# Last attention pair of a decoder step: the output layer's first operands are loaded ahead of row 7's blocks, two half tiles begin before the last values product, and the weights of the next pair are scaled behind row 1's maxima

## The chip, the cores and the metric

The kernel runs on one core of one Trainium2 chip. The metric is the device time of one execution in microseconds (us); lower is better.

## The reference

Two layers over a prompt of 1024 tokens and 8 single decode tokens: first a gated linear recurrence, then an attention layer. The change lies in the attention layer, of which this is the core:

```python
k, v = jnp.split(rms_norm(h, norm_kv) @ w_kv, 2, axis=-1)          # shared keys and values, 16 heads of 64
q, gate = jnp.split(rms_norm(x, norm_g) @ w_in, 2, axis=-1)
...
logits = jnp.where(mask, s + (c_q[..., :, None] - c_t[..., None, :]), -jnp.inf)
p = jax.nn.softmax(logits, axis=-1)
o = jnp.einsum('bhqk,bkhd->bqhd', p, v_all)
...
return x + (o * jax.nn.silu(gate)) @ w_o                           # the output layer
```

The decode tokens attend to a paged cache of 1024 keys each. All data are fp32.

## The kernel before

The first half of the run is the recurrent layer, which the change does not touch. The attention layer goes over eight pairs of heads, p = 0 to 7. A pair has eight **rows** of 128 queries (row i has i + 1 blocks of 128 keys). For a row TensorE computes scores (`scores`, L2446), VectorE adds the forget terms and takes the minimum (`row_max`, L1794 and L1798; in rows 4 to 7 also L1787), ScalarE makes the softmax (`soft`, L1274 and L1283), and the weights are transposed: rows 0 to 3 on TensorE (`turn_rows`, L2453, copied out by `turn_a` L1290 and `turn_v` L1807), rows 4 to 7 by VectorE (`turn_blocks`, L1819), stored to DRAM by SyncE (`store_row`, L679) and loaded back (`load_row`, L690). `weighted(p, m)` (L2472) multiplies rows 2m and 2m+1 with the values. `weighted(p, 3)` needs row 7's loaded blocks and stands in the next pair's row 2.

Between these the order of each engine is written by hand. In pairs 0 to 6 TensorE fills its gaps with the projections of the next pair, `kq_n` and `vg_n`: units of four matmuls (recorded as eight) at L2134, each added or copied out of one of two banks (VectorE L1451, ScalarE L1024), so that unit n waits for the taking of unit n-2. Unit 0 of `kq` waits until VectorE has scaled `w_k` and `w_q` (`scale_w`, L477, one instruction each); unit 1 waits until GpSimd has made sums of the scaled weights (`sums_of_kq`, L813 to L816, four instructions that wait for both scalings). In pair 7 there is no next pair, and `last` puts parts of the **output layer** into the gaps: `y_part(n, lo, hi)` (L2646) accumulates heads lo to hi-1 of half tile n, n = 0, 1, 2 in banks 0, 1, 7. Its first three heads wait for the semaphore `early_b`, which counts six loads: three slices of `w_o_b`, and `o_y[2]`, `o_y[0]`, `o_y[1]`. The third slice goes into the room of `c_lo[0]`, free after pair 6's last maximum, and `o_y[0]`, `o_y[1]` into `k_t[0]`, `q_t[0]`, free after pair 6's last scores.

SyncE issues all these loads from one queue in program order: `k_in` loads a page group of cached keys into a ring of two (it waits for `k_free`, which VectorE's `score`, L1873, raises after GpSimd's product `times_q`, L949), `v_in` four groups of cached values, which `decode` (L2504) reads, `hi_in(p)` (L645) the forget terms of the second half of the keys, which `row_max(p, 4)` waits for. `k_in(56)` waits until score(54) is done, and score(54) stands on VectorE behind `fin(6, 3)` (L1831), which takes the result of `weighted(6, 3)`. Behind `k_in(56)` SyncE issues three more `o_y` and `w_ob` pairs and then `hi_in(7)`. `gate_in` (L1836) is VectorE's part of the gate, behind `row_max(p, 4)`; `shift` (L1894) follows, and TensorE's `new_score` (L2491) waits for it.

Of the kernel before, what the change touches and what calls it, by code (L numbers as in the profile page):

```python
# [212 lines left out]
def build(nc, io):  # L213
    with ExitStack() as ctx:
# [340 lines left out]
        def _(sp):  # L555
# [70 lines left out]
            def k_in(*ms):  # L626

                for m in ms:
                    if m >= 2:
                        sp.wait_ge(k_free, m - 1)  # L630
                    sp.dma_start(k_ring[:, m % 2], k_pages[m % S, m // S]).then_inc(k_loaded[m % 2], 16)
# [49 lines left out]
            def load_row(p, i):  # L681
# [7 lines left out]
                src = block_rows[i - LOW_ROWS, :, 0:4 * n].rearrange("p (g n) -> p g n", g=4)  # L689
                sp.dma_start(dst, src).then_inc(pt_moved, 16)  # L690

            def pair(p):
                m = S * p
                if p:
                    k_in(m - 1)
                sp.wait_ge(b_units.done, vg_b(p, 14))
                load_wb(sp, w_v, w_kv_d, p + 1, 1, w_v_loaded)
                load_wb(sp, w_g, w_qg_d, p + 1, 1, w_g_loaded)
                if p:
                    k_in(m)  # L700
                    v_in(p - 1, 1, *range(HALF))
                    hi_in(p)
                    k_in(m + 1)
                    sp.wait_ge(max_done, 2 * TT * p)
                lo_in(p + 1)
                k_in(m + 2)
                store_row(p, 4)
                load_row(p, 4)
                k_in(m + 3)
                store_row(p, 5)  # L710
                load_row(p, 5)
                if p:
                    v_in(p, 0, 0, 1)
                k_in(m + 4)
                store_row(p, 6)
                load_row(p, 6)
                sp.wait_ge(b_units.done, kq_b(p + 1, 14))
                if p + 2 < PAIRS:
                    load_wb(sp, w_k, w_kv_d, p + 2, 0, w_k_loaded)
                    load_wb(sp, w_q, w_qg_d, p + 2, 0, w_q_loaded)  # L720
                else:
                    w_ob_in(early_b, 0, 1)
                    sp.wait_ge(ob_stored, 16 * (OWN - 1))
                    sp.dma_start(o_y[2], o_dram[2]).then_inc(early_b, 16)
                k_in(m + 5)
                store_row(p, 7)
                k_in(m + 6)
                load_row(p, 7)
                if p:
                    v_in(p, 0, 2, 3)  # L730

            def last():

                p, m = PAIRS - 1, S * (PAIRS - 1)
                k_in(m - 1)
                sp.wait_ge(max_done, 2 * TT * p)
                w_ob_in(early_b, 2)
                sp.wait_ge(s_done, scored(p - 1, TT - 1, 1))
                for h in range(2):
                    sp.dma_start(o_y[h], o_dram[h]).then_inc(early_b, 16)  # L740
                k_in(m)
                sp.wait_ge(b_units.done, vg_b(p, 14))
                sp.wait_ge(ob_stored, 16 * OWN)
                for h in range(3, OWN):
                    sp.dma_start(o_y[h], o_dram[h]).then_inc(ob_loaded[h - 3], 16)
                    w_ob_in(ob_loaded[h - 3], h)
                hi_in(p)
                w_ob_in(w_ob_loaded, AH - 2, AH - 1)
                k_in(m + 1)
                v_in(p - 1, 1, *range(HALF))  # L750
                k_in(m + 2)
                resb_in(0)
                resb_in(1)
                store_row(p, 4)
                load_row(p, 4)
                k_in(m + 3)
                store_row(p, 5)
                load_row(p, 5)
                v_in(p, 0, *range(HALF))
                k_in(m + 4)  # L760
                store_row(p, 6)
                load_row(p, 6)
                k_in(m + 5)
                store_row(p, 7)
                load_row(p, 7)
                k_in(m + 6)
                resb_in(2)
                k_in(m + 7)
                resb_in(3)
                v_in(p, 1, *range(HALF))  # L770
                for t in range(4, TT + 1):
                    resb_in(t)
# [611 lines left out]
        def _(dve):  # L1384
# [328 lines left out]
            def vg_add(p, u):  # L1713
                unit_add(vg_b(p, u), v_t, g_raw, u, b_units)
# [222 lines left out]
            for p in range(PAIRS):  # L1937
# [20 lines left out]
                    score(m - 3)  # L1958
                vg_add(p, 10)
                turn_v(p, 0)  # L1960
                if nxt:
                    scale_w(dve, w_k, gain_kv, p + 1, w_k_loaded, w_k_scaled)
                    scale_w(dve, w_q, gain_b, p + 1, w_q_loaded, w_q_scaled)
                row_max(p, 1)
                vg_add(p, 11)
                vg_add(p, 12)
                vg_add(p, 13)
                turn_v(p, 1)
                row_max(p, 2)
# [106 lines left out]
        def _(pe):  # L2076
# [435 lines left out]
            def pair(p):  # L2512
# [26 lines left out]

                scores(p, 2)  # L2540
                kq_n(0)
                if p:
                    weighted(p - 1, 3)
                kq_n(1)
                last((0, 0, 3))
                turn_values(p, 0)
                if p:
                    decode(p - 1, 0)
# [7 lines left out]
                scores(p, 3)  # L2556
                kq_n(3)
                kq_n(4)
                last((1, 0, 3))
                weighted(p, 0)  # L2560
                turn_rows(p, 3)
                if p:
# [186 lines left out]
```

## Time and profile before

| what | us |
|---|---|
| device time, median of 3 runs (1515.57 to 1516.42) | 1516.23 |
| device time of the profiled execution | 1516.44 |
| its span, from the first to the last instruction | 1514.6 |
| TensorE matmuls busy (98% of the span) | 1479.3 |
| VectorE busy (65%) | 991.3 |
| ScalarE busy (45%) | 678.2 |
| GpSimd busy (28%) | 419.9 |
| mean granted TensorE clock | 0.996 of full |

The profiled execution's time is 1.8 us over its span. Busy times of engines overlap, so they say which engine has little room, not what a change is worth; that is read from the waits at one place.

### The profile page before, as it was taken

How to read it: one execution, taken by the hardware profiler on the slowest of the kernel's cores; microseconds unless marked ns; L12 is line 12 of the kernel's file. 1: busy time of each engine (PE TensorE's matmuls, PEld its weight loads, DVE VectorE, ACT ScalarE, POOL GpSimd, SP SyncE). 2: the span in 40 equal slices, each digit the busy share in tenths (PEclk: the TensorE clock that was granted, in tenths of full speed). 3: DMA queues.
4: the chain of work that ended last, by engine and by line, in shares of the span. 5: the costliest groups of instructions: out<-in, count | busy, mean ns of one | idle time of the engine just before them, and what ended most of it. 6: DMA issues, size and time to landing. Idle time of an engine off the chain costs nothing.

```text
span 1514.6 us, 23379 instructions
## 1 busy us (share of the span) xinstructions
PE 1479.3 (98%) x8437; PEld 1090.5 (72%) x8437; DVE 991.3 (65%) x1987; ACT 678.2 (45%) x1380; POOL 419.9 (28%) x335
## 2 busy tenths in 40 slices
PE   7999999999999999999999999999999999989998
PEld 6888888888888875446777777777777777754443
DVE  6868696877868684126377677758677676748321
ACT  4445545444445552212356555546555455545100
POOL 5012322121212101012051625443452615332200
PEclk9999999999999999999999999999999999999999
DMA  9683938466483943323247779596968778698731
GB/s 268 192 240 97 292 105 260 147 190 200 150 239 99 299 155 108 102 64 128 61 124 197 251 217 305 178 279 210 280 215 248 260 229 294 185 324 315 238 134 58
DMA packets 290505, 300.53 MB, mean 198 GB/s; under 512 B 25863, under 2 KB 247295, under 8 KB 290391
## 3 DMA queue, kind: packets, MB, share of 16 engines
q1 hardware_dynamic: 279254, 262.44, 56.8%
q0 software_dynamic: 11136, 36.59, 7.1%
q8 instruction: 68, 1.11, 0.3%
q14 instruction: 47, 0.38, 0.1%
HBM read 243.57 MB, written 122.53 MB: 242 GB/s over the span
## 4 chain that ended last, share of the span: by engine, by line
PE 84%; DVE 6%; ACT 5%; DMA 2%; issue 2%; SPq 1%; POOL 0%; DVEq 0%; POOLq 0%
PE psum L2134 42%; PE psum L2158 7%; PE psum L2646 7%; PE psum L2446 4%; PE psum L2472 4%; PE psum L2211 3%; PE psum L2097 2%; PE psum L2504 2%; PE psum L2406 2%; ACT psum L1274 1%; ACT psum L1283 1%; PE psum L2281 1%; PE psum L2222 1%; PE psum L2297 1%; PE psum L2299 1%
## 5 line engine op out<-in xcount | busy, mean ns | idle before, releaser
L2134 PE MATMUL psum<-arena 128*128 128x252 f32 (+1 forms) x3472 | 811.4, 384 | 2.2 <-DVE arena L1451 2.2
L2134 PEld LDWEIGHTS psum<-arena 128*128 128x128 f32 x3472 | 640.8, 190 | 124.0 <-issue 23.1
L949 POOL TENSOR_TENSOR arena<-arena 128x1024 f32<-128x1024 f32 x64 | 158.2, 2472 | 374.2 <-DMA arena<-k_pages 368.8
L1451 DVE TENSOR_TENSOR arena<-arena,psum 128x252 f32<-128x252 f32 (+1 forms) x310 | 128.8, 416 | 160.5 <-PE psum L2134 155.7
L2646 PE MATMUL psum<-arena 128*128 128x512 f32 x256 | 115.6, 604 | 4.5 <-DMA arena<-o_heads 2.9
L2158 PE MATMUL psum<-arena 128*128 128x512 f32 x256 | 113.0, 594 | 0.1
L1024 ACT COPY arena<-psum 128x252 f32<-128x252 f32 (+1 forms) x124 | 46.2, 373 | 139.5 <-PE psum L2134 139.4
L2646 PEld LDWEIGHTS psum<-arena 128*128 128x128 f32 x256 | 47.6, 192 | 63.2 <-issue 60.7
L2158 PEld LDWEIGHTS psum<-arena 128*128 128x128 f32 x256 | 47.5, 190 | 57.4 <-issue 56.5
L1087 ACT ACTIVATE arena<-arena 128x1024 f32<-128x1024 f32 x48 | 50.7, 1056 | 84.6 <-DVE arena L1497 84.2
L1274 ACT ACTIVATE psum<-psum,arena 128x640 f32<-128x640 f32 (+3 forms) x64 | 58.9, 921 | 59.9 <-DVE arena L1798 59.9
L2446 PE MATMUL psum<-arena 64*128 64x512 f32 (+3 forms) x384 | 79.3, 516 | 2.6 <-DVE arena L1807 2.1
L1873 DVE TENSOR_REDUCE arena<-arena 128x16 f32<-128x1024 f32 x64 | 77.2, 1208 | 3.3 <-POOL arena L949 3.2
L2472 PE MATMUL psum<-arena 128*64 128x256 f32 (+1 forms) x640 | 72.0, 370 | 2.7 <-DMA arena<-block_rows 2.4
L1819 DVE STREAM_TRANSPOSE arena<-psum 128x640 f32<-128x640 f32 (+3 forms) x64 | 63.2, 1027 | 15.7 <-ACT psum L1283 15.5
L813 POOL TENSOR_TENSOR arena<-arena 128x512 f32<-128x512 f32 x31 | 40.0, 1289 | 120.3 <-PE psum L2134 106.2
L2472 PEld LDWEIGHTS psum<-arena 128*64 128x64 f32 x640 | 43.6, 137 | 38.2 <-issue 15.2
L1798 DVE CUSTOM_DVE_ANT_0 psum<-psum,arena 128x128 f32<-128x128 f32 (+3 forms) x128 | 63.7, 534 | 2.2
L2211 PEld LDWEIGHTS psum<-arena 128*128 128x128 f32 x448 | 58.1, 191 | 4.7 <-issue 2.1
L1787 DVE CUSTOM_DVE_ANT_0 psum<-psum,arena 128x512 f32<-128x512 f32 x64 | 42.9, 710 | 28.3 <-PE psum L2446 28.1
L2446 PEld LDWEIGHTS psum<-arena 64*128 64x128 f32 x384 | 32.5, 185 | 39.3 <-issue 37.8
L2211 PE MATMUL psum<-arena 128*128 128x128 f32 x448 | 59.9, 277 | 0.0
(272 smaller groups left out, 2086.4 us busy)
## 6 DMA issues: line engine op xcount, KB each, us to landing
k_pages<-in_cache_k SPq DMA_DIRECT2D x64, 512.0 KB, 6.5
v_pages<-in_cache_v SPq DMA_DIRECT2D x64, 512.0 KB, 7.2
arena<-k_pages SPq DMA_DIRECT2D x64, 512.0 KB, 5.3
arena<-v_pages SPq DMA_DIRECT2D x64, 512.0 KB, 6.8
arena<-in_w_in_a SPq DMA_DIRECT2D x32, 512.0 KB, 6.9
arena<-in_x_prompt SPq DMA_DIRECT2D x16, 512.0 KB, 7.5
arena<-in_w_kv SPq DMA_DIRECT2D x16, 512.0 KB, 6.6
arena<-in_w_in_b SPq DMA_DIRECT2D x16, 512.0 KB, 7.6
```

The source lines that it names most:

```text
L949: pool.tensor_tensor(k_ring[:, m % 2], k_ring[:, m % 2], q_all[:, m % S:m % S + 1, :].broadcast_to([P, PAGES, P]), ALU.mult).then_inc(kq_m ...
L1274: ins = act.activation(dst[:, x, 0:n], rows[:, x, 0:n], ACT.Exp, bias=top[:, at:at + 1], scale=-1.0, accum_out=total[:, at:at + 1])
L1451: dve.tensor_tensor(out, more, bank[n % 2][:, 0:size(u)], ALU.add).then_inc(of.by_dve, 1)
L1798: dve.tensor_tensor_reduce(out=rows[:, x, lo:n], in0=rows[:, x, lo:n], in1=c, scale=1.0, scalar=part[:, at:at + 1] if lo else -LOW, op0=AL ...
L1819: dve.transpose(out, row_banks(i)[:, x, 0:(i + 1) * P].rearrange("p (j r l) -> p j r l", r=4, l=32)).then_inc(blocks_turned, 1)
L1873: dve.tensor_reduce(lg[:, b, :, 0:PAGES].rearrange("p x j -> p j x"), k_ring[:, m % 2].rearrange("p j (x d) -> p j x d", x=2), AX.X, ALU.a ...
L2134: ins = pe.matmul(bank[n % 2][:, 0:size(u)], w[:, k, :], x[:, k, :], start=(k == 0 and r in (0, 1, 3, 4)), stop=(k == HK - 1), skip_group_ ...
L2158: ins = pe.matmul(dst[0:rows, :], o_heads[h][:, rows_of(t)], w_o[:, h, 512 * j:512 * j + 512], start=(h == 0 or lo == AH - 1), stop=(h == ...
L2211: ins = pe.matmul(bank[2 + l % 2][:, i * P:(i + 1) * P], f[:, i * P:(i + 1) * P], q[:, i], start=True, stop=True)
L2446: ins = pe.matmul(dst[:, x, lo:hi], q_t[p % 2][rows, cols(i)], k_t[p % 2][rows, lo:hi], start=True, stop=True)
L2472: ins = pe.matmul(bank[6][rows, lo:2 * P], v_cur[:, j, rows], moving(m, x, j), start=(j == 0), stop=(j == i), skip_group_check=True)
L2646: ins = pe.matmul(dst, o_y[h][:, cols(t)], w_ob[h][:, 512 * j:512 * j + 512], start=(h == 0), stop=(h == AH - 1), skip_group_check=True)
```

## The change

It has three parts.

1. SyncE, pair 6: the third slice of `w_ob` and `o_y[0]`, `o_y[1]` (`ob_early`) are issued behind `store_row(6, 7)` and ahead of `load_row(6, 7)`, and `k_in(54)` behind that load. Before, they were issued at the start of `last`, behind `load_row(6, 7)`, two `v_in` loads and `k_in(55)`.
2. TensorE, pair 7: `y_part` for the first three heads of half tiles 0 and 1 stands ahead of `weighted(6, 3)` in row 2. Before, half tile 0 stood behind it, and half tile 1 in row 3, ahead of `weighted(7, 0)`.
3. VectorE, pairs 0 to 6: the two scalings of `w_k` and `w_q` stand behind `row_max(p, 1)` and the takings of units 11 and 12, instead of ahead of `row_max(p, 1)`.

```diff
+            def ob_early(p):
+                sp.wait_ge(max_done, 2 * TT * (p + 1))
+                w_ob_in(early_b, 2)
+                sp.wait_ge(s_done, scored(p, TT - 1, 1))
+                for h in range(2):
+                    sp.dma_start(o_y[h], o_dram[h]).then_inc(early_b, 16)
+
             def pair(p):
...
                 store_row(p, 7)
-                k_in(m + 6)
-                load_row(p, 7)
+                if p + 2 == PAIRS:
+                    ob_early(p)
+                    load_row(p, 7)
+                    k_in(m + 6)
+                else:
+                    k_in(m + 6)
+                    load_row(p, 7)
                 if p:
                     v_in(p, 0, 2, 3)
...
                 k_in(m - 1)
-                sp.wait_ge(max_done, 2 * TT * p)
-                w_ob_in(early_b, 2)
-                sp.wait_ge(s_done, scored(p - 1, TT - 1, 1))
-                for h in range(2):
-                    sp.dma_start(o_y[h], o_dram[h]).then_inc(early_b, 16)
                 k_in(m)
...
                 turn_v(p, 0)
+                row_max(p, 1)
+                vg_add(p, 11)
+                vg_add(p, 12)
                 if nxt:
                     scale_w(dve, w_k, gain_kv, p + 1, w_k_loaded, w_k_scaled)
                     scale_w(dve, w_q, gain_b, p + 1, w_q_loaded, w_q_scaled)
-                row_max(p, 1)
-                vg_add(p, 11)
-                vg_add(p, 12)
                 vg_add(p, 13)
...
                 scores(p, 2)
                 kq_n(0)
+                last((0, 0, 3), (1, 0, 3))
                 if p:
                     weighted(p - 1, 3)
                 kq_n(1)
-                last((0, 0, 3))
                 turn_values(p, 0)
...
                 kq_n(4)
-                last((1, 0, 3))
                 weighted(p, 0)
```

TensorE's order in pair 7, from row 2's scores (L2446) to row 3's, before:

```order
L2446 MATMUL psum<-arena 128x384 x2
L2472 MATMUL psum<-arena 64x256 x14
L2472 MATMUL psum<-arena 64x128 x2
L2646 MATMUL psum<-arena 128x512 x3
L2426 MATMUL psum<-arena 128x128 x4
...
L2446 MATMUL psum<-arena 128x512 x2
L2646 MATMUL psum<-arena 128x512 x3
L2472 MATMUL psum<-arena 64x256 x2
```

And in the changed kernel, where lines from 692 on stand up to seven further down (L2453 is `scores`, L2652 `y_part`, L2479 `weighted`):

```order
L2453 MATMUL psum<-arena 128x384 x2
L2652 MATMUL psum<-arena 128x512 x6
L2479 MATMUL psum<-arena 64x256 x14
L2479 MATMUL psum<-arena 64x128 x2
L2433 MATMUL psum<-arena 128x128 x4
...
L2453 MATMUL psum<-arena 128x512 x2
L2479 MATMUL psum<-arena 64x256 x2
```

Both output parts now stand ahead of `weighted(6, 3)`, and none stands between row 3's scores and `weighted(7, 0)`.

SyncE's order of loads around row 7 of pair 6, before:

```order
L679 DMA block_rows<-arena 32x4x512 x4
L631 DMA arena<-k_pages 128x1024
L690 DMA arena<-block_rows 128x4x512
L637 DMA arena<-v_pages 128x1024 x2
L631 DMA arena<-k_pages 128x1024
L663 DMA arena<-in_w_o_b 128x1024
L740 DMA arena<-o_heads 128x1032 x2
L631 DMA arena<-k_pages 128x1024
```

And in the changed kernel (L697 is in `ob_early`):

```order
L679 DMA block_rows<-arena 32x4x512 x4
L663 DMA arena<-in_w_o_b 128x1024
L697 DMA arena<-o_heads 128x1032 x2
L690 DMA arena<-block_rows 128x4x512
L631 DMA arena<-k_pages 128x1024
L637 DMA arena<-v_pages 128x1024 x2
L631 DMA arena<-k_pages 128x1024 x2
```

Three loads instead of one now stand between row 7's store and its load.

VectorE's order in rows 0 and 1 of a pair (pair 0 here; pairs 1 to 6 change alike), before:

```order
L1807 COPY arena<-psum 128x128
L477 TENSOR_TENSOR arena<-arena 128x1024 x2
L1794 TENSOR_TENSOR psum<-psum,arena 128x2x128
...
L1451 TENSOR_TENSOR arena<-arena,psum 128x264 x3
L1807 COPY arena<-psum 128x256
```

And in the changed kernel (L1801 is `row_max`, L1458 the taking of a unit, L1814 `turn_v`):

```order
L1814 COPY arena<-psum 128x128
L1801 TENSOR_TENSOR psum<-psum,arena 128x2x128
...
L1458 TENSOR_TENSOR arena<-arena,psum 128x264 x2
L477 TENSOR_TENSOR arena<-arena 128x1024 x2
L1458 TENSOR_TENSOR arena<-arena,psum 128x264
L1814 COPY arena<-psum 128x256
```

The scalings moved behind the first two of the three takings.

## Rows read from the trace of the kernel before

**Rows 1.** The page's engine totals and its chain that ended last

```profile
PE 1479.3 (98%) x8437; PEld 1090.5 (72%) x8437; DVE 991.3 (65%) x1987; ACT 678.2 (45%) x1380; POOL 419.9 (28%) x335
PE 84%; DVE 6%; ACT 5%; DMA 2%; issue 2%; SPq 1%; POOL 0%; DVEq 0%; POOLq 0%
```

**Rows 2.** TensorE's timeline in pair 7: start, length, count, [idle before, releaser]

```profile
1343.20 0.92 PE L2446 MATMUL psum<-arena 64*128 64x384 f32 x4
1346.12 5.18 PE L2472 MATMUL psum<-arena 128*64 128x256 f32 x32 [2.00 <-DMA arena<-block_rows]
1354.24 4.23 PE L2646 MATMUL psum<-arena 128*128 128x512 f32 x6 [2.94 <-DMA arena<-o_heads]
1358.31 0.60 PE L2426 MATMUL psum<-arena 128*128 128x128 f32 x4
...
1363.25 1.13 PE L2446 MATMUL psum<-arena 64*128 64x512 f32 x4
1364.31 2.84 PE L2646 MATMUL psum<-arena 128*128 128x512 f32 x6
1367.42 0.87 PE L2472 MATMUL psum<-arena 128*64 128x256 f32 x8 [0.27 <-DVE arena L1921]
...
1377.95 0.40 PE L2491 MATMUL psum<-arena 128*128 128x16 f32 x2 [1.26 <-DVE arena L1894]
```

**Rows 3.** Two windows: length, engines' busy times, granted clock, DMA share, GB/s

```profile
1339.00:1340.00 1.00, 1.00 (x6) 0.84 (x5) 0.43 (x1) 0.90 (x5) 0.80 (x2) 1.00 0.51 63
1346.10:1351.30 5.20, 5.18 (x32) 3.00 (x32) 0.00 (x0) 1.96 (x6) 2.23 (x2) 0.67 1.02 409
```

**Rows 4.** SyncE's timeline of DMA issues at the same place

```profile
1334.23 0.84 SPq L631 DMA_DIRECT2D arena<-k_pages  x1
1337.43 0.53 SPq L690 DMA_DIRECT2D arena<-block_rows  x1
...
1340.55 0.48 SPq L663 DMA_DIRECT2D arena<-in_w_o_b  x1
1341.07 1.12 SPq L740 DMA_DIRECT2D arena<-o_heads  x2
1352.93 0.32 SPq L631 DMA_DIRECT2D arena<-k_pages  x1
...
1357.39 0.45 SPq L645 DMA_DIRECT2D arena<-c_rows  x1
```

**Rows 5.** The DMA view: issues, KB each, us to landing

```profile
arena<-c_rows SPq DMA_DIRECT2D x1, 512.0 KB, 11.4
```

**Rows 6.** VectorE's timeline in pair 7, row 4

```profile
1373.03 0.46 DVE L1794 TENSOR_TENSOR psum<-psum,arena 128x256 f32<-128x256 f32 x1
...
1374.07 3.35 DVE L1836 SCALAR_TENSOR_TENSOR arena<-arena 128x1032 f32<-128x1032 f32 x1
```

**Rows 7.** GpSimd's timeline in the same row

```profile
1373.99 2.34 POOL L949 TENSOR_TENSOR arena<-arena 128x1024 f32<-128x1024 f32 x1 [8.62 <-DMA arena<-k_pages]
```

**Rows 8.** VectorE's timeline in pair 0, rows 0 to 1

```profile
756.75 2.35 DVE L477 TENSOR_TENSOR arena<-arena 128x1024 f32<-128x1024 f32 x2
...
761.47 0.43 DVE L1451 TENSOR_TENSOR arena<-arena,psum 128x264 f32<-128x264 f32 x1 [0.85 <-PE psum L2134]
```

**Rows 9.** GpSimd's timeline in pair 0

```profile
759.91 1.28 POOL L813 TENSOR_TENSOR arena<-arena 128x512 f32<-128x512 f32 x1
...
763.84 1.27 POOL L816 TENSOR_TENSOR arena<-arena 128x512 f32<-128x512 f32 x1
```

**Rows 10.** TensorE's timeline in pair 0, row 2

```profile
764.36 3.67 PE L2134 MATMUL psum<-arena 128*128 128x252 f32 x16
767.86 0.60 PE L2426 MATMUL psum<-arena 128*128 128x128 f32 x4
```

**Rows 11.** Pair 6, rows 1 to 2: TensorE's timeline, with VectorE's taking of unit 12

```profile
1256.64 0.43 DVE L1451 TENSOR_TENSOR arena<-arena,psum 128x264 f32<-128x264 f32 x1 [0.85 <-PE psum L2134]
1258.15 0.60 PE L2453 MATMUL psum<-arena 128*128 128x128 f32 x4
1259.52 1.97 PE L2134 MATMUL psum<-arena 128*128 128x252 f32 x8
1261.42 3.53 PE L2472 MATMUL psum<-arena 128*64 128x256 f32 x32
1264.88 1.97 PE L2134 MATMUL psum<-arena 128*128 128x252 f32 x8
```

## The prediction

> **What bounds the kernel now.** I read the page first: TensorE is busy 98% of the span and holds 84% of the chain that ended last [rows 1]. So an edit pays only where TensorE stands still or runs at a low clock, and it costs wherever it makes TensorE wait. Next I read TensorE's timeline where the change moves its work, in pair 7. There it stands 2.00 us for row 7's blocks and, after `weighted(6, 3)`, 2.94 us for `o_heads` [rows 2]. The same product took 3.53 us in pair 6 [rows 11] and takes 5.18 here [rows 2]; the window over it shows a granted clock of 0.67, a mix of the two levels of 2.4 and 1.2 GHz [rows 3]. The first output part takes 4.23 us, the second, at full clock, 2.84 [rows 2]. So this place holds 4.94 us of standing and 1.65 + 1.39 = 3.04 us of half clock. The third reading is TensorE around the scalings, in pair 0 and in pair 6 [rows 10, 11]: no idle stands there.
>
> **Part 1, the loads.** Before, the third `w_ob` slice is issued at 1340.55, the two `o_heads` from 1341.07 [rows 4], and the wait for them ends at 1354.24 [rows 2], behind 1 MB of row blocks, 1 MB of values and 512 KB of keys at some 409 GB/s [rows 3]. Now their 1.58 MB stand right behind the store, from about 1334. The store is done by 1337.43, when the row's load is issued [rows 4]. At 409 GB/s 1.58 MB are 3.9 us, and the queue starts slowly after the store, so I take them as landed at 1343 (bounds 1342.3 to 1344.3). TensorE can use them from 1343.20 + 0.92 = 1344.1. The row blocks stood behind 512 KB of keys and now stand behind 1.58 MB: 1.06 MB more, 2.6 us at that rate if nothing was idle. But from 1339 to 1340 the DMA share was 0.51 at 63 GB/s [rows 3], a hole that the extra bytes fill. So the blocks land 0.4 to 3 us later than 1346.12; I take 1 us, 1347.1.
>
> By the Trainium skill (DMA: Bandwidth & Descriptors, "Queues, rings and completion order") each DMA engine takes a queue's descriptors in ring order, so a load moved ahead is paid by all behind it. The landing order here, blocks before `o_heads`, agrees. Without the hole the rule alone gives the blocks 2.6 us later, at 1348.7, and the sum stays as it is, since 1349.7 below is later still.
>
> **Part 2, TensorE.** The two output parts run from 1344.1, 2 × 2.8 = 5.6 us at full clock, to 1349.7. They cover the wait for the blocks (1347.1, at most 1349.1). `weighted(6, 3)` then takes 3.5 us at full clock, to 1353.2. Before, the next work began at 1358.31 [rows 2]. Gain there: **5.1 us** (4.6 if the operands are half a microsecond late), all of the standing and all of the half clock, less the part taken over from row 3.
>
> Row 3 gives something back without cost: between its scores (end 1364.3) and `weighted(7, 0)` at 1367.42 lay the second part, 2.84 us [rows 2]. `weighted(7, 0)` waits for VectorE, so this becomes a hole of about 3 us. A hole of 2.00 us was followed by 1346.1 to 1351.3 at 0.67 [rows 2, 3], so a half clock stretch is likely after it, up to 1.6 us.
>
> What is late next is `hi_in(7)`. `weighted(6, 3)` now ends at 1353.2 instead of 1351.3; behind it on VectorE stand `fin(6, 3)` and score(54), and behind those SyncE's `k_in(56)`, at 1352.93 before [rows 4], now 1354.8. So everything queued behind is 1.9 us later. The forget terms were issued at 1357.39 [rows 4] and took 11.4 us [rows 5], landing at 1368.8; now 1370.7. Row 4's second half began at 1373.03 [rows 6]; 5.1 us earlier would be 1367.9. It can't start before 1370.8, so the lead falls to 2.2 us there, and the half clock stretch above is hidden in this wait.
>
> Then some of it returns. `gate_in` took 3.35 us [rows 6] because GpSimd's product began at 1373.99 [rows 7], 0.08 us before it. Alone I estimate 1.2 us, since a scaling of nearly its size takes half of 2.35 [rows 8]. GpSimd's product waits for keys that the full queue brings no earlier than before, so now `gate_in` runs at about 1371.8 to 1373.0, ahead of it. That returns 2.1 us: `new_score` starts at 1373.8 instead of 1377.95 [rows 2], a lead of **4.1 us**. By the Trainium skill (SBUF: State Buffer, "SBUF: two separate sides") a VectorE operation with two SBUF inputs and a GpSimd operation exclude each other for a whole instruction; 3.35 against 1.2 us agrees. TensorE reaches that wait early and stands about 2.3 us, which may again bring a half clock stretch, 0 to 1.6 us; I take 0.8. The rest of the pair is output work without idle, so the lead is kept. Pair 7: **-3.3 us** (bounds -5.1, all kept, and -1.4, `gate_in` caught again and a clock stretch).
>
> **Part 3, the scalings.** In pair 0 unit 12 is taken at 761.47 [rows 8]. The scalings start 0.35 us later and take 2.35 [rows 8]: done at 764.17. GpSimd's four sums took 765.11 - 759.91 = 5.20 us [rows 9]: done at 769.4 instead of 765.1. Unit 0 of `kq` starts at 764.36 [rows 10], just behind the scalings. Unit 1 starts half way through the 3.67 us, at 766.2, because in pair 0 no `weighted(p - 1, 3)` stands between the two. It now waits till 769.4: 3.2 us. Nothing else of TensorE's can go ahead; everything behind is late alike, but for 0.2 us of a wait on ScalarE. So **+3.0 us** (bounds 2.8 and 3.3). The hole is longer than the 2.00 us that was followed by a low clock; a stretch in which half the speed is lost costs 0 to 1.65, and I take +1.0.
>
> In pairs 1 to 6 the product stands between the units. In pair 6 unit 12 is taken at 1256.64, the scalings are done at 1259.35, unit 0 starts at 1259.52; the sums are done at 1264.6, unit 1 starts at 1264.88 [rows 11]. The margins are 0.2 and 0.3 us. Cost nothing, bound 0.4 us a pair; together I take +0.2 (0 to 2.4). The earlier row 1 maxima gain nothing: `turn_rows(p, 1)` at 1258.15 [rows 11] stands behind three units and is reached without idle. Delayed too are GpSimd's products behind the sums (by 3.5 us) and so score(8p - 2) and `k_in(8p)` (by 1.7); VectorE next waits for `decode` anyway.
>
> Sum: -3.3 + 3.0 + 1.0 + 0.2 = **+0.9 us**. The profiled execution took 1516.44, 0.2 over the median of 1516.23; from the median, 1517.1.
>
> **The rivals.** *The lead of pair 7 is not returned* (slower): `gate_in` is caught by GpSimd's product again, or the forget terms land later still, and the lead stays near 1.4 us. Decides if GpSimd's next product starts before VectorE's `gate_in` ends. Then -1.4 + 4.2 = +2.8, and with thin margins failing by 0.3 in six pairs +4.6: 1519 to 1521. For it: the margins of 0.2 us and a full queue; against it: the keys' place in the queue. *The earlier row maxima carry through* (faster): if `soft(p, 1)` being done 1.6 to 2.3 us earlier released TensorE in each of seven pairs by even 0.7 us, that is -4.9, total -4.0: 1512.2. It decides from about 0.6 us a pair. Against it: no idle in rows 0 to 2 of pair 6 [rows 11]. *Pair 0 doesn't wait* (no change or faster): if the sums were not late, -3.3 + 0.2 = -3.1, 1513.1. Against it stand the four sums' 5.20 us, which can't fit between 764.2 and 766.2. *The loads come no earlier* (the change doesn't do what it says): `early_b` still ends the wait after 1349; pair 7 gains under 1 us, total +4, 1520. Against it: no other bytes stand ahead of them but the store.
>
> **How the numbers follow.** A measurement of this kernel can tell about 0.2%, 3.0 us, from no change. Forecast, both effects as worked out: 0.57, time 1517.1, own range 1514.5 to 1519.2. Lead not returned, or thin margins failing: 0.22. Loads no earlier: 0.05. Row maxima carry through, or pair 0 not late: 0.13. Something unseen: 0.03. Of the forecast's share 0.04 falls on each side beyond 3.0 us. Faster 0.17, same 0.55, slower 0.28. The range that leaves out 2 in 10 is 1513.0 to 1520.8.
>
> **What the changed profile would show.** In pair 7 the first output parts start within 0.5 us of row 2's scores and run as x12 in 5.6 us; `weighted(6, 3)` follows without idle in 3.5 us; a hole of 3 us in row 3; row 4's second half waits for `c_rows`; `gate_in` near 1.2 us. In pair 0 unit 1 waits 3.2 us for L816. In pairs 1 to 6 no wait for L477 or L816 over 0.3 us. I am wrong if pair 0 shows no hole, if a wait for row 7's blocks stays, or if row 4 takes the whole lead.

## The result, and the profile after

The changed kernel is **slower by 0.33%**: 1520.5 us (median of 7, 1519.09 to 1523.81) against 1516.4 us (median of 7) for the kernel before on the same chip, ratio 1.0033 [1.0021, 1.0045]. The forecast was 1517.1. The profiled execution is the fastest of the seven, 1519.09 us with a span of 1517.3, against 1516.44 and 1514.6 before. It therefore shows only 2.65 of the 4.1 us between the medians.

In this kernel.py the lines stand up to 7 further down: L2141 is the unit that was L2134, L2453 the scores, L2479 `weighted`, L2652 the output part, L2498 `new_score`, L823 the last sum, L956 GpSimd's product.

**Pair 0.** TensorE's timeline after the change, to be held against [rows 10]:

```profile
765.16 1.97 PE L2141 MATMUL psum<-arena 128*128 128x252 f32 x8
770.35 2.46 PE L2141 MATMUL psum<-arena 128*128 128x252 f32 x8 [3.21 <-POOL arena L823]
772.60 1.06 PE L2433 MATMUL psum<-arena 128*128 128x128 f32 x4
773.46 1.48 PE L2460 MATMUL psum<-arena 128*128 128x128 f32 x6
```

What ran as one group of 16 in 3.67 us [rows 10] is now cut in two by a hole of 3.21 us, and what follows the hole is slow: eight matmuls take 2.46 us instead of 1.97. GpSimd's and VectorE's rows give the reason (against [rows 8, 9]):

```profile
762.28 0.43 DVE L1458 TENSOR_TENSOR arena<-arena,psum 128x264 f32<-128x264 f32 x1 [1.35 <-PE psum L2141]
762.62 2.35 DVE L477 TENSOR_TENSOR arena<-arena 128x1024 f32<-128x1024 f32 x2
...
765.12 1.26 POOL L820 TENSOR_TENSOR arena<-arena 128x512 f32<-128x512 f32 x1 [4.41 <-issue]
...
769.02 1.27 POOL L823 TENSOR_TENSOR arena<-arena 128x512 f32<-128x512 f32 x1
```

The scalings end at 764.97, the sums begin 0.15 us later and end at 770.29, and unit 1 starts at 770.35.

**Pair 7, TensorE** (against [rows 2]; row 2's scores now start 5.34 us later in the span, at 1348.54 instead of 1343.20; 4.5 of it come from pair 0, 0.8 were there ahead of it):

```profile
1348.54 0.92 PE L2453 MATMUL psum<-arena 64*128 64x384 f32 x4
1349.39 5.42 PE L2652 MATMUL psum<-arena 128*128 128x512 f32 x12
1354.73 3.53 PE L2479 MATMUL psum<-arena 128*64 128x256 f32 x32
1358.19 0.66 PE L2433 MATMUL psum<-arena 128*128 128x128 f32 x4
...
1363.41 1.13 PE L2453 MATMUL psum<-arena 64*128 64x512 f32 x4
1368.64 1.55 PE L2479 MATMUL psum<-arena 128*64 128x256 f32 x8 [4.10 <-DVE arena L1928]
1370.12 1.97 PE L2460 MATMUL psum<-arena 128*128 128x128 f32 x8
...
1379.15 0.29 PE L2498 MATMUL psum<-arena 128*128 128x16 f32 x2
...
1381.51 1.56 PE L2453 MATMUL psum<-arena 64*128 64x512 f32 x8 [1.11 <-DVE arena L1826]
1383.00 2.84 PE L2652 MATMUL psum<-arena 128*128 128x512 f32 x6
1386.15 0.39 PE L2506 MATMUL psum<-arena 128*128 128x8 f32 x2 [0.31 <-DVE arena L1908]
```

Row 2 is what was meant: twelve matmuls, then the product, nothing between, all at full speed. Row 3 has a hole of 4.10 us, and behind it eight small matmuls (L2460) take 1.97 us where the same eight take 1.27 before. The windows (length, busy times, granted clock, DMA share, GB/s) show the clock in both places:

```profile
770.30:774.90 4.60, 4.55 (x19) 4.10 (x20) 0.42 (x1) 1.07 (x2) 2.23 (x3) 0.65 0.41 138
...
1365.00:1372.00 7.00, 3.36 (x17) 2.66 (x18) 5.38 (x15) 3.78 (x9) 3.75 (x3) 0.54 0.98 352
```

A granted clock of 0.65 and 0.54 is mostly the lower level, 1.2 GHz, each time with TensorE idle just before or during the window.

**VectorE and GpSimd in pair 7** (against [rows 6, 7]):

```profile
1365.19 2.33 POOL L956 TENSOR_TENSOR arena<-arena 128x1024 f32<-128x1024 f32 x1 [3.77 <-DMA arena<-k_pages]
...
1379.81 2.34 POOL L956 TENSOR_TENSOR arena<-arena 128x1024 f32<-128x1024 f32 x1 [10.87 <-DMA arena<-k_pages]
...
1366.32 1.22 DVE L1926 TENSOR_TENSOR arena<-arena 64x4 f32<-64x4 f32 x1
1367.57 0.15 DVE L1927 TENSOR_TENSOR arena<-arena,psum 64x4 f32<-64x4 f32 x1
...
1376.93 1.23 DVE L1843 SCALAR_TENSOR_TENSOR arena<-arena 128x1032 f32<-128x1032 f32 x1
...
1382.18 1.22 DVE L1880 TENSOR_REDUCE arena<-arena 128x16 f32<-128x1024 f32 x1 [0.72 <-POOL arena L956]
```

`gate_in` fell from 3.35 to 1.23 us, since GpSimd's product no longer starts with it. But the overlap has moved rather than gone: the `smp_out` product L1926, a 64x4 operation that takes 0.16 us in its second turn (1367.94), now meets GpSimd's earlier product and takes 1.22. That is 1.06 us of row 3's hole.

**A table by stage.** The quickest way to see where time goes in pair after pair is the distance from one row's first scores on TensorE to the next row's (for a whole pair, from its row 0 to the next pair's). In us, each from one profiled execution:

| kernel | pair 0 | pair 7 row 2 | row 3 | row 4 | row 5 | rows 2 to 5 |
|---|---|---|---|---|---|---|
| before | 75.7 | 20.05 | 7.33 | 8.86 | 12.56 | 48.8 |
| after | 80.3 | 14.87 | 9.80 | 8.30 | 13.14 | 46.1 |

Pairs 1 to 6 together take 503.95 before and 503.97 after. So the profile's sum is +4.5 in pair 0 and -2.7 in pair 7. The other 0.9 us of the 2.65 between the times lie outside the stretches that the change touches (0.8 of them ahead of pair 0, whose first scores start at 752.21 instead of 751.40); they are of the size by which two executions of one kernel differ here (1515.23 to 1517.21 before).

### The profile page after: what moved, and what is told of

It is laid out like the page before. It is cut to its first block, busy times and chain, and to the rows that moved or that the text cites. A ratio compares the mean times of both kernels' runs of the same rounds, so it can differ in the third digit from the quotient of the medians.

```text
span 1517.3 us, 23379 instructions
## 1 busy us (share of the span) xinstructions
PE 1480.8 (98%) x8437; PEld 1092.9 (72%) x8437; DVE 993.4 (65%) x1987; ACT 678.1 (45%) x1380; POOL 417.4 (28%) x335
## 3 DMA queue, kind: packets, MB, share of 16 engines
q8 instruction: 68, 1.11, 0.3%
## 4 chain that ended last, share of the span: by engine, by line
PE 87%; DVE 6%; ACT 4%; issue 2%; DMA 1%; POOL 1%; SPq 0%; DVEq 0%; POOLq 0%
PE psum L2141 44%; PE psum L2165 7%; PE psum L2652 7%; PE psum L2453 5%; PE psum L2479 4%; PE psum L2218 3%; PE psum L2511 2%; PE psum L2104 2%; PE psum L2413 2%; ACT psum L1281 1%; PE psum L2304 1%; PE psum L2229 1%; PE psum L2288 1%; ACT psum L1290 1%; PE psum L2460 1%
## 5 line engine op out<-in xcount | busy, mean ns | idle before, releaser
L2141 PE MATMUL psum<-arena 128*128 128x252 f32 (+1 forms) x3472 | 812.2, 385 | 5.4 <-POOL arena L823 3.2
L2141 PEld LDWEIGHTS psum<-arena 128*128 128x128 f32 x3472 | 641.5, 190 | 127.0 <-issue 22.1
L956 POOL TENSOR_TENSOR arena<-arena 128x1024 f32<-128x1024 f32 x64 | 156.3, 2442 | 354.8 <-DMA arena<-k_pages 352.2
L1458 DVE TENSOR_TENSOR arena<-arena,psum 128x252 f32<-128x252 f32 (+1 forms) x310 | 128.9, 416 | 165.8 <-PE psum L2141 163.6
L2652 PE MATMUL psum<-arena 128*128 128x512 f32 x256 | 114.1, 598 | 1.6 <-DVE arena L1872 1.6
L2652 PEld LDWEIGHTS psum<-arena 128*128 128x128 f32 x256 | 47.4, 191 | 59.5 <-issue 56.9
L2453 PE MATMUL psum<-arena 64*128 64x512 f32 (+3 forms) x384 | 79.3, 517 | 3.3 <-DVE arena L1814 1.9
L2479 PE MATMUL psum<-arena 128*64 128x256 f32 (+1 forms) x640 | 71.0, 367 | 4.1 <-DVE arena L1928 4.1
L1826 DVE STREAM_TRANSPOSE arena<-psum 128x640 f32<-128x640 f32 (+3 forms) x64 | 63.2, 1026 | 16.2 <-ACT psum L1290 16.2
L2479 PEld LDWEIGHTS psum<-arena 128*64 128x64 f32 x640 | 43.1, 136 | 39.1 <-issue 19.3
L2453 PEld LDWEIGHTS psum<-arena 64*128 64x128 f32 x384 | 32.4, 185 | 40.1 <-issue 37.6
```

The lines of the kernel that those rows point to most:

```text
L956: pool.tensor_tensor(k_ring[:, m % 2], k_ring[:, m % 2], q_all[:, m % S:m % S + 1, :].broadcast_to([P, PAGES, P]), ALU.mult).then_inc(kq_m ...
L1458: dve.tensor_tensor(out, more, bank[n % 2][:, 0:size(u)], ALU.add).then_inc(of.by_dve, 1)
L1826: dve.transpose(out, row_banks(i)[:, x, 0:(i + 1) * P].rearrange("p (j r l) -> p j r l", r=4, l=32)).then_inc(blocks_turned, 1)
L2141: ins = pe.matmul(bank[n % 2][:, 0:size(u)], w[:, k, :], x[:, k, :], start=(k == 0 and r in (0, 1, 3, 4)), stop=(k == HK - 1), skip_group_ ...
L2453: ins = pe.matmul(dst[:, x, lo:hi], q_t[p % 2][rows, cols(i)], k_t[p % 2][rows, lo:hi], start=True, stop=True)
L2479: ins = pe.matmul(bank[6][rows, lo:2 * P], v_cur[:, j, rows], moving(m, x, j), start=(j == 0), stop=(j == i), skip_group_check=True)
```

## The experiments

Each is told by its edit against the kernel named. Ratios are to the kernel before, timed beside it on the same chip; gains in us that are said to be timed are worked out from them. Different runs were on different chips, so runs are compared by their ratios and not by their medians.

### Pair 0 against the other pairs

**e1**: the kernel before with part 3 alone, in all pairs (the hunk shown in the change). 

> Part 3 alone, in all seven pairs; loads and output parts stand as before. Theory A (pair 0 holds the cost: 3.2 us of standing for the sums, about 1.3 us of half clock behind it, nothing in pairs 1 to 6): +4.5 us, 1520.9. Theory B (the thin margins of 0.2 to 0.3 us in pairs 1 to 6 fail in most executions, though not in the profiled one): +6 us or more, and over the kernel that moves pair 0's scalings alone by 1.5 us or more. Theory C (pair 7 gains less in most executions than the 2.6 us of the profiled one) says nothing here.

Measured: 1521.49, ratio 1.0030 [1.0018, 1.0042].

**e4**: the same in pair 0 alone.

```
                turn_v(p, 0)
-               if nxt:
+               late = p == 0
+               if nxt and not late:
                    scale_w(...)
                row_max(p, 1)
...
+               if nxt and late:
+                   scale_w(...)
```

> The kernel before with the scalings moved in pair 0 alone. Theories A and C: +4.5 us, 1520.9, all that part 3 costs. Theory B: +4.5 us too, but 1.5 us or more below part 3 in all pairs. If the half clock behind the hole is there in only some executions, the times spread between +3.2 and +4.9 us.

Measured: 1521.16, 1.0031 [1.0021, 1.0041]. Pair 0 takes 80.3 us in e4, 80.4 in e1 and 75.7 before. TensorE's timeline of e4:

```profile
764.67 1.97 PE L2138 MATMUL psum<-arena 128*128 128x252 f32 x8
769.85 2.64 PE L2138 MATMUL psum<-arena 128*128 128x252 f32 x8 [3.22 <-POOL arena L816]
772.29 1.06 PE L2430 MATMUL psum<-arena 128*128 128x128 f32 x4
```

**e3**: the changed kernel with pair 0 alone put back (`late = p > 0`). 

> The changed kernel with pair 0's scalings back in their old place, those of pairs 1 to 6 moved. Theory A: -2.6 us against before, as parts 1 and 2 alone; 1513.8. Theory B: 0 us or slower. Theory C: -1 to +0.5 us, again as parts 1 and 2 alone.

Measured: 1516.64, 0.9996 [0.9987, 1.0005]; pair 0 takes 75.6 us again.

**e2**: the changed kernel without part 3. 

> Parts 1 and 2 alone; the scalings stand as before. Theories A and B: pair 7 gains what the profile of the changed kernel shows, -2.6 us, 1513.8. Theory C (pair 7's gain is mostly lost in most executions, to VectorE's and GpSimd's exclusion and to half clock behind the hole in row 3): between -1 and +0.5 us.

Measured: 1515.39, 0.9992 [0.9983, 1.0001].

What follows: moving the scalings in pair 0 alone costs as much as moving them in all seven pairs (+4.7 and +4.5 us by the ratios). Each of these figures is uncertain by 1.5 us and more; the traces say it more sharply: in the changed kernel and in e1 the 3.2 us of pair 0 are the only wait for the sums or the scalings that TensorE's timeline shows from pair 0 to pair 6. So the thin margins of 0.2 and 0.3 us in the other pairs held, and that theory falls. The cost is the 3.2 us wait and about 1.3 us of low clock behind it. And parts 1 and 2 bring only 1.2 us (-0.2 to 2.6), where the profile of e2 shows 2.4 in rows 2 to 5 and 3.3 were forecast.

### Where the lead of row 2 goes

**e7**: part 1 alone (e2, with both half tiles where the kernel before has them).

```
-                last((0, 0, 3), (1, 0, 3))
...
                kq_n(1)
+                last((0, 0, 3))
                turn_values(p, 0)
...
                kq_n(4)
+                last((1, 0, 3))
                weighted(p, 0)
```

> Part 1 alone: loads early, both output parts where they stood, scalings as before. Theory D: TensorE waits for row 7's blocks about 1 us longer than before (3 us), the product runs half clocked, the parts no longer wait: rows 2 to 5 some 46 us, -2.5 us. Rival F (the order of the parts is the whole gain, the loads move nothing): the wait for the blocks grows by what the wait for the operands loses, 0 us.

Measured: 1515.34, 0.9995 [0.9986, 1.0004]. In its profile TensorE waits 3.48 us for row 7's blocks instead of 2.00, and no longer for `o_heads`.

**e5**: e2 with the second half tile back in row 3, so that no hole is left there.

```
-                last((0, 0, 3), (1, 0, 3))
+                last((0, 0, 3))
...
                kq_n(4)
+                last((1, 0, 3))
                weighted(p, 0)
```

> Scalings as before, loads early, only half tile 0 ahead of the last values product; half tile 1 back in row 3. Theory D (row 3's hole, which the second part filled before, is what gives the lead back: rows 3 to 4 took 2.5 to 3.2 us longer in the three profiles of kernels with both parts ahead): row 3 takes 7.3 us again, rows 2 to 5 some 44 us against 48.8 to 49.8 before and 46.1 to 46.7 with both parts ahead; -4.5 us, 1512.5. Rival E (the forget terms of row 4 and the keys bound row 4, whatever fills row 3): row 3 short, row 4 longer by as much, total as with both parts ahead, -1 to -2.5 us.

Measured: 1514.13, 0.9985 [0.9976, 0.9994].

**e6**: e5, with the forget terms of pair 7 issued earlier in SyncE's queue.

```
                k_in(m)
+                hi_in(p)
...
                    w_ob_in(ob_loaded[h - 3], h)
-                hi_in(p)
```

> As the kernel with only half tile 0 ahead, and the forget terms for row 4 loaded right behind the keys of group 56, ahead of the six output operands. Theory D: same as without that move within 1 us. Rival E: 2 us faster or more than without that move.

Measured: 1512.93, 0.9981 [0.9972, 0.9990].

**e8**: the same edit on e2. 

> Both parts ahead and loads early, scalings as before, and the forget terms early. Theory D: row 3 stays long (about 10 us), the total as with parts 1 and 2 alone within 1 us. Rival E: faster than parts 1 and 2 alone by 1.5 us or more.

Measured: 1514.31, 0.9988 [0.9979, 0.9997].

The stage table goes on:

| kernel | row 2 | row 3 | row 4 | row 5 | rows 2 to 5 |
|---|---|---|---|---|---|
| e2 | 14.87 | 10.53 | 8.26 | 12.72 | 46.4 |
| e7 | 17.13 | 7.34 | 9.36 | 13.14 | 47.0 |
| e5 | 13.61 | 7.34 | 11.02 | 14.50 | 46.5 |
| e6 | 12.94 | 7.33 | 9.19 | 15.72 | 45.2 |
| e8 | 14.87 | 8.58 | 8.07 | 17.06 | 48.6 |

Row 3's hole can be had back (e5: 7.34), yet rows 2 to 5 last as long: rows 4 and 5 take what row 3 gives. (One profile settles no difference under some 2 us: e8's rows are 2.2 us longer than e2's, and by the ratios it is 0.6 us faster.) In e5 VectorE waits in row 4 for the forget terms, and what TensorE does behind that wait is slow (row 5's scores take 2.93 us instead of 1.56, the output parts after them 3.41 instead of 2.84); these 1.94 us are all that row 5 is longer by:

```profile
1369.60 0.43 DVE L1801 TENSOR_TENSOR psum<-psum,arena 128x256 f32<-128x256 f32 x1 [2.84 <-DMA arena<-c_rows]
```

In e6 the terms are early and this wait is gone. TensorE then waits for an output block, VectorE for GpSimd's product, that product for keys (TensorE's, VectorE's and GpSimd's timelines of e6):

```profile
1369.78 1.98 PE L2653 MATMUL psum<-arena 128*128 128x512 f32 x4 [1.80 <-DMA arena<-in_w_o_b]
...
1376.02 1.22 DVE L1880 TENSOR_REDUCE arena<-arena 128x16 f32<-128x1024 f32 x1 [4.41 <-POOL arena L956]
...
1373.65 2.34 POOL L956 TENSOR_TENSOR arena<-arena 128x1024 f32<-128x1024 f32 x1 [13.15 <-DMA arena<-k_pages]
```

The product starts at 1373.65 here, at 1374.91 in e2 and at 1373.99 before [rows 7], although TensorE's row 3 scores start 7.0 us earlier in e6 than before (1356.25 against 1363.25 [rows 2]). A point in time that stays put while everything ahead of it moves is the mark of another resource. Two theories were left for it: the order of SyncE's queue, or the number of bytes.

### Order or bytes

**e9**: e6, with the keys of group 57 ahead of output blocks 6 and 7. **e10**: these blocks behind the values and the keys of group 58 too. **e11**: e9's edit on e2.

```
-                w_ob_in(w_ob_loaded, AH - 2, AH - 1)
                k_in(m + 1)
+                w_ob_in(w_ob_loaded, AH - 2, AH - 1)
                v_in(p - 1, 1, *range(HALF))
```

> The kernel of e6 (loads early, both part groups as in e5, softmax terms of pair 7 early) with one more edit: SyncE issues the keys of group 57 ahead of output blocks 6 and 7 (1 MB) instead of behind them. In e6 these keys were issued at 1361.56 us, as soon as the score of group 55 had freed their buffer, and the product on GpSimd started at 1373.65, 12 us later; the score of 57 then held row 5's maxima 4.41 us and the decode 2.89 us. Theory 'the order of the queue holds rows 4 and 5': the product starts 2 to 3 us earlier, near 1371, row 5 of pair 7 falls from 15.7 to about 13.1, and the time falls by about 2.5 us against e6, to 1510.5. Theory 'the lead is lost on the engines and the keys are only the last of several waits': the product moves, but another wait (for output operands or a half-speed clock) takes the place, and the time stays within 1 us of e6's 1512.9.

Measured: 1514.14, 0.9982 [0.9972, 0.9992].

> As e9, but output blocks 6 and 7 are issued still later, behind the values of pair 6 and the keys of group 58 as well. Queue-order theory: nothing in rows 4 and 5 waits for these, so rows 4 and 5 are as in e9, and the time is the same as e9's within 0.5 us, unless blocks 6 and 7 are then late for row 5's parts, which would show as a wait of TensorE for in_w_o_b behind row 5's scores. Theory of several waits: as e6 within 1 us.

Measured: 1516.28, 1.0003 [0.9993, 1.0012].

> The changed kernel without its scalings (e2: both first half tiles in row 2), with the keys of group 57 ahead of output blocks 6 and 7. Queue-order theory: the hole in row 3 stays (10 us), but the product starts 2 to 3 us before 1374.9, the 0.9 and 0.7 us waits behind it go, and the time falls by 1 to 1.5 us against e2's 1515.4. Theory that the lead of e2 is lost in row 3's hole alone: no change from e2 within 0.5 us.

Measured: 1516.74, 1.0007 [0.9998, 1.0016].

The queue-order theory forecast 1510.5 for e9 and a gain of 1 to 1.5 us over e2 for e11. Both missed. For e10 it forecast e9's time, unless the blocks came late and TensorE waited for them behind row 5's scores; that is what came. Row 5 of e10 takes 20.2 us:

```profile
1380.11 3.78 PE L2653 MATMUL psum<-arena 128*128 128x512 f32 x4 [4.62 <-DMA arena<-in_w_o_b]
```

In e9 the product did move, from 1373.65 to 1369.27, and rows 4 and 5 fell from 24.9 to 22.9 us, most of the 2.5 that the theory gave them. Then row 6 grew from 13.18 to 16.61. TensorE waits for no load there (e9's VectorE, GpSimd and TensorE in row 6):

```profile
1389.19 1.89 DVE L1926 TENSOR_TENSOR arena<-arena 64x4 f32<-64x4 f32 x1
...
1388.73 2.34 POOL L956 TENSOR_TENSOR arena<-arena 128x1024 f32<-128x1024 f32 x1 [8.17 <-DMA arena<-k_pages]
...
1393.02 8.83 PE L2653 MATMUL psum<-arena 128*128 128x512 f32 x16 [3.30 <-DVE arena L1872]
```

The small operation L1926 meets GpSimd's product again, as in row 3 of the changed kernel, and takes 1.89 us; in e6 it takes 0.15 there. TensorE stands 3.30 us instead of 1.57, and the sixteen matmuls behind take 8.83 us instead of 7.13, at a granted clock of 0.81 from 1393 to 1402 us, where e6 has 1.00. These two differences are 1.73 and 1.70 us, all that row 6 grew by. So e9 doesn't refute the theory of the order: without this meeting its rows would be 3.4 us shorter. Nothing was run that takes it away.

e11 is no faster than e2 (1.0007 against 0.9992), though its product came 2.5 us earlier too: row 3 is 2.0 us shorter (8.50, with no meeting of L1926 and the product), and then VectorE waits in row 4 for the forget terms (2.50 us), with the clock low behind. These terms stand ahead of the moved keys in the queue, so this is not a price of the move; the shorter row 3 no longer hides them.

A load that is put back can be missed, as e10 shows. By the Trainium skill (DMA: Bandwidth & Descriptors, "Queues, rings and completion order") each DMA engine takes a queue's descriptors in ring order; e10, with 4.62 us at the blocks that were put back, agrees. For the theory of the bytes the windows of e6 have the numbers:

```profile
1350.00:1355.00 5.00, 5.00 (x92) 3.91 (x89) 2.39 (x6) 1.07 (x2) 4.14 (x3) 1.00 0.63 179
1355.00:1380.00 25.00, 19.24 (x85) 8.70 (x83) 16.54 (x45) 13.34 (x28) 6.71 (x6) 1.00 1.01 394
```

For 25 us the DMA engines are full, at 394 GB/s; in the 5 us ahead they move 179. SyncE issues nothing from 1341 until 1352.72, because it stands at the keys of group 56, whose buffer is still in use, with some 4 MB of output operands behind them (three heads and five blocks of 0.5 MB). In e12 the first of these could be issued at 1342.52.

**e12**: e6, with output operands 3 and 4 ahead of that wait (`ob_in` issues the two loads of the old loop for each head named).

```
                k_in(m - 1)
-                k_in(m)
-                hi_in(p)
                sp.wait_ge(b_units.done, vg_b(p, 14))
                sp.wait_ge(ob_stored, 16 * OWN)
-                for h in range(3, OWN):
-                    sp.dma_start(o_y[h], o_dram[h]).then_inc(ob_loaded[h - 3], 16)
-                    w_ob_in(ob_loaded[h - 3], h)
...
+                ob_in(3, 4)
+                k_in(m)
+                hi_in(p)
+                ob_in(5)
```

> The kernel of e6 with output operands 3 and 4 (heads and weight blocks) issued ahead of the keys of group 56, that is near 1344 us instead of 1353.7. In all kernels so far the DMA engines move 143 to 233 GB/s in 1350 to 1355 us and then 350 to 417 GB/s for 25 us; moving the keys of 57 ahead of blocks 6 and 7 (e9) took 1.9 us off rows 4 and 5 and cost 3.4 in row 6. Theory 'full engines': what holds rows 4 to 6 is the sum of bytes behind 1355, not their order; here about 1 MB of it moves into the gap, so 1 to 2.5 us: the product of group 57 starts near 1371 instead of 1373.7, TensorE's 1.80 us wait for an output block goes, row 5 falls from 15.7 to 13.1 to 14.2 with row 6 still 13.2, and the time falls to 1509.5 to 1511.5. Theory 'order of the queue': keys of 56 come behind more bytes, the score of 56 is late and row 4 pays it; the time stays at e6's 1512.9 or above.

Measured: **1509.45** (1506.32 to 1509.7, 5 runs), 0.9948 [0.9935, 0.9962]. Faster than both kernels, and than before by 7.9 us (5.8 to 9.9) by the ratio, 6.5 by the medians; the theory of full engines forecast 1509.5 to 1511.5. Its windows, and TensorE's and GpSimd's rows with waits from row 3's scores to row 6's, all there are:

```profile
1350.00:1355.00 5.00, 5.00 (x91) 3.88 (x87) 2.61 (x6) 1.07 (x2) 3.94 (x3) 1.00 1.02 410
1355.00:1380.00 25.00, 23.02 (x153) 11.59 (x152) 21.05 (x49) 16.67 (x35) 9.13 (x6) 1.00 0.96 377
```

```profile
1360.19 0.87 PE L2484 MATMUL psum<-arena 128*64 128x256 f32 x8 [0.27 <-DVE arena L1933]
1371.60 1.56 PE L2458 MATMUL psum<-arena 64*128 64x512 f32 x8 [0.89 <-DVE arena L1831]
...
1359.63 2.35 POOL L961 TENSOR_TENSOR arena<-arena 128x1024 f32<-128x1024 f32 x1 [3.90 <-DMA arena<-k_pages]
1369.04 2.34 POOL L961 TENSOR_TENSOR arena<-arena 128x1024 f32<-128x1024 f32 x1 [5.64 <-DMA arena<-k_pages]
1375.96 2.44 POOL L961 TENSOR_TENSOR arena<-arena 128x1024 f32<-128x1024 f32 x1 [4.58 <-DMA arena<-k_pages]
```

The idle 5 us now carry 410 GB/s. The keys of group 56 do come later (their product at 1359.63 instead of 1356.74), but nothing waited for it; the keys of group 57 come 4.6 us earlier, although their place in the queue is the same as in e6.

**e13** and **e14**: bytes taken away instead of moved, on the kernel before and on e2. Only the first half of the columns of output operands 3 to 5 and of blocks 6 and 7 is loaded, some 2 MB less; that part of the output layer's data is left out, with the same instructions and waits.

```
-                    sp.dma_start(o_y[h], o_dram[h]).then_inc(ob_loaded[h - 3], 16)
-                    w_ob_in(ob_loaded[h - 3], h)
+                    sp.dma_start(o_y[h][:, 0:N // 2], o_dram[h][:, 0:N // 2]).then_inc(ob_loaded[h - 3], 16)
+                    w_half_in(ob_loaded[h - 3], h)
...
-                w_ob_in(w_ob_loaded, AH - 2, AH - 1)
+                w_half_in(w_ob_loaded, AH - 2, AH - 1)
```

> The kernel before, but of output operands 3 to 5 and of output weight blocks 6 and 7 only the first half of the columns is loaded (the rest keeps what the buffers held: part of the computation is left out). Same number of transfers, waits and instructions, some 2 MB less to move in rows 3 to 5. Theory 'full engines': without the lead of part 1 little is gained in rows 3 and 4, because TensorE's own work sets them; row 5 is 12.6 already; at most 1 us faster than before. Base for the next run.

Measured: 1516.75, 1.0005 [0.9995, 1.0014].

> The changed kernel without its scalings (e2), with the same halves left out as in e13 (part of the computation is left out). Theory 'full engines': the lead of row 2 (5.2 us) is now carried through rows 4 to 6 except for what row 3's hole takes (2 to 3 us): 2 to 4 us faster than e13, where e2 was 0.7 to 2.3 us faster than before. If the lead is lost on the compute engines alone, the difference between this and e13 stays at 1 to 1.5 us.

Measured: 1512.91, 0.9978 [0.9969, 0.9987].

| kernel | row 2 | row 3 | row 4 | row 5 | rows 2 to 5 |
|---|---|---|---|---|---|
| e9 | 12.81 | 7.34 | 8.69 | 14.22 | 43.1, row 6 +3.4 |
| e12 | 13.17 | 7.51 | 8.07 | 12.56 | 41.3 |
| e13 | 20.79 | 7.33 | 8.07 | 12.56 | 48.8 |
| e14 | 14.88 | 8.59 | 8.07 | 12.56 | 44.1 |
| e11 | 14.87 | 8.50 | 10.68 | 15.14 | 49.2 |

With fewer bytes the same parts 1 and 2 are worth 4.1 us (1.0005 - 0.9978 = 0.0027 of 1516; 2.1 to 6.1), with all bytes 1.2 (-0.2 to 2.6). On the kernel before the same bytes are worth nothing that can be measured. The clearest comparison is that of e14 with e8 and e11: all three have both parts ahead, the same row 2 (14.87 or 14.88) and nearly the same row 3 (8.50 to 8.59), and then rows 4 and 5 together take 20.6 us with fewer bytes, and 25.1 (e8) and 25.8 (e11) with all of them. So the lead needs room behind it on the DMA engines, and 8.07 and 12.56 us are what rows 4 and 5 take when nothing is late.

## Why the prediction was wrong

**What held.** The blocks of row 7 come later as said: with only one part ahead of them TensorE waits for them until 1347.57 in e6 (1347.1 said, at most 1349.1). The parts run as x12 in 5.42 us behind row 2's scores and `weighted(6, 3)` follows in 3.53 us (5.6 and 3.5 said). Unit 1 of pair 0 waits 3.21 us for the last sum (3.2 said). The margins of pairs 1 to 6 held. `gate_in` takes 1.23 us (1.2 said). `new_score` starts at 1379.15; less the 5.34 us that row 2 starts later this is 1373.81, a lead of 4.1 us, as forecast. (The working had 2.2 + 2.1 for it, which are 4.3.)

**Right number, wrong way.** That the lead of 4.1 us came out is luck. I had row 3's hole hidden in a wait of row 4 for `hi_in(7)`. In the changed kernel that wait doesn't show at all. The hole itself took the lead (row 3 is 2.5 us longer), being 4.10 us and not 3: 1.06 us by the exclusion of L1926 and GpSimd's product, and then at low clock. In e8, e11 and e14, where the product ends before L1926 starts, the hole is 3.04 or 3.05 us. The late terms stood hidden behind it; in e5, where the hole is gone, they show as 2.84 us. Two limits lay on top of each other, so removing one (e5, e8) gave about 1 us or less against e2.

The 2.1 us that `gate_in` was to return are no fixed price either. In e1 and e4, whose pair 7 has the instructions of the kernel before, GpSimd's product starts 1.9 and 1.7 us ahead of `gate_in`, which then takes 1.58 and 1.71 us and not 3.35, and row 4 takes 8.07 us and not 8.86. One profiled execution had been read as if every one were like it.

**The step that failed: "The rest of the pair is output work without idle, so the lead is kept. Pair 7: -3.3 us".** It isn't without idle. First TensorE stands 1.11 us ahead of row 5's scores for VectorE's transposes (L1826), which themselves wait 1.24 us for ScalarE: the lead falls from 4.1 to 3.3 us. Then comes row 5. I had written that GpSimd's product waits for keys "that the full queue brings no earlier than before", and used it for `gate_in` alone; the same product also releases score(57), which row 5 needs. So row 5 is 0.6 us longer in the changed kernel (0.72 us of waiting for the product), and 3.2 and 4.5 us longer in e6 and e8, where VectorE waits 4.41 and 2.99 us for it. The lead at row 6 is 2.7 us. The term measured -2.7 us in the profiled execution, and parts 1 and 2 alone -1.2 us (-2.6 to +0.2) when timed. Behind it stands what e12 to e14 show: the DMA engines are full for 25 us, and the lead of row 2 isn't carried through this stretch unless bytes are moved ahead of it or left out.

**A term that was too small.** Pair 0: +3.0 and +1.0 forecast, 4.5 us in the stage table and +4.7 us (3.2 to 6.2) timed in e4. The standing was right; the low clock behind it cost about 1.3 us.

With the two terms as timed, -1.2 + 4.7 = +3.5 us, against 0.9 forecast and 4.1 measured by the medians (5.0 by the ratio, 3.2 to 6.8). The rival "lead of pair 7 not returned" has the right size (1519 to 1521) but not the right cause: `gate_in` was not caught again, and the thin margins held.

**Open.** Why e2's timed gain (1.2) is smaller than its profile's (2.4) isn't settled; its interval reaches 2.6. Why the keys of group 56 come late enough for the meeting in row 3 in the changed kernel, e2 and e3, and not in e8, e11 and e14, wasn't found. What e9's order is worth without the meeting in row 6 wasn't run. How much of e12's 7.9 us is the wait for the output block in row 4 and how much the keys of group 57 wasn't taken apart: both went at once.

## What to carry to other kernels

Before counting a lead that loads at the front of a stretch give you, look at the DMA rate of the whole stretch behind: where it is full, a lead on the compute engines is easily lost again. Here bytes moved into an idle window ahead of it (or left out) kept the lead; no other order of the queue gained anything clear of noise, though e9's was not tried without its accident in row 6. Look for that window in front of a wait at the head of the queue: a load that waits for its buffer keeps others back whose buffers are long free. A step that is moved "behind" a small one in a loop over pairs is to be followed in the first pair by itself, where the work that gives the others their margin is missing.

## What was not expected of the hardware

A 64x4 operation of VectorE on two SBUF operands that lasts 0.16 us took 1.22 us when it started 1.1 us into a GpSimd product of 2.33 us; its end is that product's end. So it did in row 6 of e9: 1.89 us, started 0.46 us into a product of 2.34. The overlap costs the rest of the longer instruction, not a share of the shorter one's length. The Trainium skill's rule (SBUF: State Buffer, "SBUF: two separate sides"), that the two exclude each other for a whole instruction, agrees; what I hadn't seen is that it makes even the smallest operation worth placing.

The DMA engines kept up 394 GB/s over 25 us, and there a load's time to landing went with the bytes ahead of it: keys of 512 KB issued at 1361.56 in e6 released their product at 1373.65, 12.1 us later, and in e12, issued at 1361.33, at 1369.04, 7.7 us later.
